# First two column steps of a Fourier projection and of an MLP quarter: weights loaded as 256 by 1024 and multiplied column by column alternately

## The reference

```
sh1, sc1, g1, sh2, sc2, g2 = split(silu(c) @ w_mod + b_mod, 6)
h = modulate(rms_norm(x, norm_g[0]), sh1, sc1)
y = fourier_mix(h) @ fnet_w_out                    # 2048 x 2048
x = x + g1 * rms_norm(y, norm_g[1])
h2 = modulate(rms_norm(x, norm_g[2]), sh2, sc2)
x = x + g2 * rms_norm(square(relu(h2 @ w_mlp_in)) @ w_mlp_out, norm_g[3])   # 2048 -> 8192 -> 2048
```

## Time and profile before

| | us |
|---|---|
| median of 3 runs | 2063.47 (2063.24 to 2064.76) |
| time of the profiled execution | 2066.94 |
| its span | 2064.8 |
| PE busy in it | 2008.3 |
| DVE busy in it | 1437.5 |

### The profile page before, as it was taken

The page is one execution under the profiler, slowest core; times in us unless marked ns, Lnnn a source line. Parts: engine busy times, 40 slices in busy tenths (PEclk is TensorE's granted clock), DMA queues, the critical chain, the costliest instruction groups (busy, mean ns, idle before and its releaser), DMA issues.

```text
span 2064.8 us, 23217 instructions
## 1 busy us (share of the span) xinstructions
PE 2008.3 (97%) x8825; PEld 1628.3 (79%) x8825; DVE 1437.5 (70%) x1507; ACT 1065.6 (52%) x1376; POOL 206.4 (10%) x407
## 2 busy tenths in 40 slices
PE   3999999999999999999999999999999999999998
PEld 1777568888888888888788888888888888888887
DVE  7989867656665555556646566756687887978875
ACT  3333535545444544544666755555555655656554
POOL 0000012001100200200001110000003113031130
PEclk9999999999999999999999999999999999999999
DMA  9999998878866656765555555456656657566573
GB/s 399 402 394 373 352 368 260 293 240 268 284 227 192 215 203 193 222 206 175 173 194 184 176 179 189 160 181 200 229 196 211 227 193 232 197 204 234 193 248 119
DMA packets 210425, 484.41 MB, mean 235 GB/s; under 512 B 17648, under 2 KB 26288, under 8 KB 201488
## 3 DMA queue, kind: packets, MB, share of 16 engines
q1 hardware_dynamic: 196048, 463.25, 65.6%
q0 software_dynamic: 13104, 16.27, 2.7%
q10 hardware_dynamic: 1168, 3.46, 0.4%
HBM read 459.84 MB, written 2.10 MB: 224 GB/s over the span
## 4 chain that ended last, share of the span: by engine, by line
PE 85%; DMA 6%; DVE 6%; ACT 2%; issue 1%; ACTq 0%; DVEq 0%
PE ps L604 23%; PE ps L606 23%; PE ps L605 23%; PE ps L635 4%; PE ps L636 4%; PE ps L634 4%; DVE scr L1672 3%; DMA raw<-in_w_mod 2%; DMA raw<-in_fnet_w 2%; DVE w_low L1659 2%; DMA raw<-in_w_mlp_in 2%; ACT w_high L1148 1%; DVE scr L1687 1%; PE ps L755 1%; PE ps L796 0%
## 5 line engine op out<-in xcount | busy, mean ns | idle before, releaser
L1659 DVE TENSOR_TENSOR w_low<-raw,w_high 128x1024 fp32r<-128x1024 f32 x464 | 563.7, 1222 | 419.9 <-ACT w_high L1148 419.6
L1148 ACT ACTIVATE w_high<-raw 128x1024 fp32r<-128x1024 f32 x464 | 486.7, 1058 | 584.2 <-PE ps L606 480.7
L604 PE MATMUL ps<-w_high,h_both 128*128 128x512 f32 x1152 | 457.4, 397 | 8.8 <-DVE w_low L1659 7.2
L605 PE MATMUL ps<-w_low,h_both 128*128 128x512 f32 x1152 | 450.6, 391 | 0.0
L606 PE MATMUL ps<-w_high,h_both 128*128 128x512 f32 x1152 | 450.5, 391 | 0.0
L604 PE MATMUL ps<-w_high,u_high 128*128 128x512 f32 x1152 | 449.6, 390 | 0.7 <-DVE u_low L2280 0.7
L606 PE MATMUL ps<-w_high,u_low 128*128 128x512 f32 x1152 | 448.6, 389 | 0.0
L605 PE MATMUL ps<-w_low,u_high 128*128 128x512 f32 x1152 | 448.5, 389 | 0.0
L1277 ACT ACTIVATE w_high<-raw 128x1024 fp32r<-128x1024 f32 x232 | 245.2, 1060 | 234.7 <-PE ps L606 117.6
L1862 DVE TENSOR_TENSOR w_low<-raw,w_high 128x1024 fp32r<-128x1024 f32 x232 | 283.1, 1221 | 95.7 <-ACT w_high L1277 91.2
L604 PEld LDWEIGHTS ps<-w_high,h_both 128*128 128x128 f32 x1152 | 217.6, 189 | 58.8 <-DVE w_low L1659 7.7
(11 more groups left out here) (227 smaller groups left out, 1563.9 us busy)
## 6 DMA issues: line engine op xcount, KB each, us to landing
raw<-in_w_mod SPq DMA_DIRECT2D x96, 1024.0 KB, 7.4
raw<-in_w_mlp_in SPq DMA_DIRECT2D x64, 1024.0 KB, 5.7
raw<-in_w_mlp_out SPq DMA_DIRECT2D x64, 1024.0 KB, 5.3
raw<-in_w_up SPq DMA_DIRECT2D x64, 1024.0 KB, 5.1
raw<-in_w_down SPq DMA_DIRECT2D x64, 1024.0 KB, 5.1
raw<-in_w_in SPq DMA_DIRECT2D x48, 1024.0 KB, 5.1
raw<-in_fnet_w SPq DMA_DIRECT2D x16, 1024.0 KB, 7.3
raw<-in_w_out SPq DMA_DIRECT2D x16, 1024.0 KB, 5.0
```

What stands on the lines that cost most here:

```text
L604: eng.matmul(dst, ah, wh, start=(k == first), stop=False)
L605: eng.matmul(dst, ah, wl, start=False, stop=False)
L1148: eng.activation(w_high[:, h % LEAD, :], raw[:, slot, (h % 2) * 2 * CW:(h % 2 + 1) * 2 * CW], ACT.Copy).then_inc(high_ready, 1)
L1659: eng.tensor_tensor(w_low[:, h % LEAD, :], raw[:, slot, piece], w_high[:, h % LEAD, :].bitcast(f32), ALU.subtract).then_inc(raw_used if h ...
```

## The change

For FNET and for the first MLP quarter, column steps 0 and 1 are loaded together: a piece now holds 256 rows by 1024 columns instead of 512 by 512 (`column_pair`), so a contiguous run in memory is 4 KB instead of 2 KB. Each piece is still 1 MB and still gives two halves, but these are now the same two row tiles for step 0 and for step 1. The order of products follows: (0, hh), (1, hh) alternate, so step 0 ends at index 14 of FNET instead of 7, and step 1 at 15 as before. Steps 2 and 3 are as they were. In the MLP, steps 1 and 2 swap banks (4 and 2), and the indices of the blocks and takes move.

```diff
-FIRST_ORDER = [(c, hh) for half in range(2) for c in range(UP_FIRST) for hh in range(4 * half, 4 * half + 4)] + \
+FIRST_ORDER = [pair for half in range(2) for pair in
+               [(c, hh) for hh in range(4 * half, 4 * half + 4) for c in range(2)] +
+               [(2, hh) for hh in range(4 * half, 4 * half + 4)]] + \
               [(c, hh) for c in range(UP_FIRST, NC) for hh in range(HALVES)] + DOWN_ORDER
 FIRST_CHUNKS = [(c, hh // 2) for c, hh in FIRST_ORDER[::2]]
+FNET_ORDER = [(c, hh) for hh in range(HALVES) for c in range(2)] + [(c, hh) for c in (2, 3) for hh in range(HALVES)]
+FNET_ENDS = {FNET_ORDER.index((c, HALVES - 1)): c for c in range(NC)}
+FIRST_PAIRS = {y // 2: hh for y, (c, hh) in enumerate(FIRST_ORDER) if c == 0}
+PAIRED = {y for y, (c, _) in enumerate(FNET_ORDER + FIRST_ORDER) if c < 2}
-FIRST_BANK = (0, 2, 4, 2, 0, 2, 0, 2)
+FIRST_BANK = (0, 4, 2, 4, 0, 2, 0, 2)
-FIRST_TAKES = {y + d: c for c, (y, d) in enumerate(zip(FIRST_UP_ENDS, (5, 6, 7, 6)))}
-FIRST_BLOCKS = {y + d: c for c, (y, d) in enumerate(zip(FIRST_UP_ENDS, (0, 1, 2, 0)))}
+FIRST_TAKES = {y + d: c for c, (y, d) in enumerate(zip(FIRST_UP_ENDS, (4, 7, 7, 6)))}
+FIRST_BLOCKS = {y + d: c for c, (y, d) in enumerate(zip(FIRST_UP_ENDS, (0, 3, 3, 0)))}
...
+            def column_pair(w, hh):
+                load(w[2 * hh * P:2 * (hh + 1) * P, 0:2 * CW].rearrange("(k p) n -> p k n", p=P), 2)
...
             def first_chunk(ch):
+                if ch in FIRST_PAIRS:
+                    column_pair(w_mlp_in, FIRST_PAIRS[ch])
+                    return
...
-                if unit == FNET:
+                if unit == FNET and k < HALVES:
+                    column_pair(fnet_w, k)
+                elif unit == FNET:
                     chunk(fnet_w, k % 4 * 4 * P, k // 4 * CW)
...
-            for c in range(NC):
-                if c >= 2:
+            for y, (c, hh) in enumerate(FNET_ORDER):
+                ch = y // 2
+                if c >= 2 and hh == 0:
                     eng.wait_ge(summed, c - 1)
...
-                eng.activation(w_high[:, h % LEAD, :], raw[:, slot, (h % 2) * 2 * CW:(h % 2 + 1) * 2 * CW],
-                               ACT.Copy).then_inc(high_ready, 1)
+                if h in PAIRED:
+                    eng.activation(ring(w_high, h % LEAD, 2), raw_blocks(slot, EIGHT, h % 2), ACT.Copy)\
+                       .then_inc(high_ready, 1)
...
                 if y < NC * HALVES - LEAD:
                     fnet_high()
-                if y % HALVES == 7:
-                    c = y // HALVES
-                    t.add("done", 8)
+                if y in FNET_ENDS:
+                    c = FNET_ENDS[y]
+                    t.c["done"] = y + 1
                     t.add("summed")
```

More of the change, by code:

```diff
@@ L451, in _ @@
                     mod_tile(G2, MOD_FIRST.index(pos))
-                for c, y in enumerate(FIRST_UP_ENDS):
+                for y, c in FIRST_BLOCKS.items():
                     if pos + 2 == y // 2 + EXCHANGED_BEHIND - 1:
@@ L899, in _ @@
             eng.wait_ge(shift_added, 1)
-            for c in range(NC):
-                if c >= 2:
+            for y, (c, hh) in enumerate(FNET_ORDER):
+                ch = y // 2
+                if c >= 2 and hh == 0:
                     eng.wait_ge(summed, c - 1)
[L903 to L914, removed]
+                if ch == 4 * NC - 1 and y % 2 == 0:
+                    eng.wait_ge(mod_cols, 3)
+                    bias_rows(SC2A)
+                if y % 2 == 0:
+                    t.c["raw"] = AT[FNET, ch]
+                half(2 * (c % 2), hh, h_high, h_low)
+                if y % 2 and ch == GATE_ROWS:
+                    last_read(G1)
+                    sum_partitions_to_rows(G1)
+            t.add("summed", NC)
             for r in range(ROWS_ON_PE):
@@ L940, in _ @@
                 elif hh == 0 and c in (4, 5):
-                    eng.wait_ge(up_taken, 1 if c == 4 else 4)
+                    eng.wait_ge(up_taken, 1 if c == 4 else 3)
                 elif hh == 0 and c > 5:
@@ L1147, in high_part @@
                     eng.wait_ge(half_used, t.at("high", 1 - LEAD))
-                eng.activation(w_high[:, h % LEAD, :], raw[:, slot, (h % 2) * 2 * CW:(h % 2 + 1) * 2 * CW],
-                               ACT.Copy).then_inc(high_ready, 1)
+                if h in PAIRED:
+                    eng.activation(ring(w_high, h % LEAD, 2), raw_blocks(slot, EIGHT, h % 2), ACT.Copy)\
+                       .then_inc(high_ready, 1)
+                else:
+                    eng.activation(w_high[:, h % LEAD, :], raw[:, slot, (h % 2) * 2 * CW:(h % 2 + 1) * 2 * CW],
+                                   ACT.Copy).then_inc(high_ready, 1)
                 t.add("high")
@@ L1658, in low_part @@
                 eng.wait_ge(high_ready, t.at("low", 1))
-                eng.tensor_tensor(w_low[:, h % LEAD, :], raw[:, slot, piece], w_high[:, h % LEAD, :].bitcast(f32),
-                                  ALU.subtract).then_inc(raw_used if h % 2 else low_first, 1)
+                done = raw_used if h % 2 else low_first
+                if h in PAIRED:
+                    eng.tensor_tensor(ring(w_low, h % LEAD, 2), raw_blocks(slot, EIGHT, h % 2),
+                                      ring(w_high, h % LEAD, 2).bitcast(f32), ALU.subtract).then_inc(done, 1)
+                else:
+                    eng.tensor_tensor(w_low[:, h % LEAD, :], raw[:, slot, piece], w_high[:, h % LEAD, :].bitcast(f32),
+                                      ALU.subtract).then_inc(done, 1)
                 t.add("low")
```

## The result

| | before | after |
|---|---|---|
| median, us | 2065.18 (6 runs beside it, 2063.24 to 2067.99) | 2073.29 (6 runs, 2071.74 to 2077.68) |
| ratio | | 1.0037 [1.0026, 1.0049] |
| profiled execution, us | 2066.94 | 2071.74 |
| its span, us | 2064.8 | 2069.9 |

The ratio is worth +7.6 us (2065.2 x 0.0037), with an interval of +5.4 to +10.1. The prediction said +2.7 on a median of 2063.47 (three runs, now 2065.18 over six), and 2069.3 at the most. The sign of the likeliest case held; the time lies outside the range.

The account below looks back on a forecast made before the run. Loads near their limit bounded the first 300 us, with DMA, DVE and PE within a few per cent in the Fourier product; PE bounded the rest. 2.1 + 1.7 - 0.9 - 0.2 = +2.7 us gave 2066.2 us, range 2060.7 to 2069.3.

Parts of the forecast that it names:

- the likeliest case: Fourier half 16: PE's wait outweighs the loads' gain; 2063.5 to 2067.5 us, point 2066.2; chance 0.50.
- The rest ... I take 0: MLP order and step ends: later h tiles and ACT's wait for transposes, about 1 us, change nothing; 0 us.
- With no PE wait of note from 305 us on I take 0.: Behind 305 us: PE's longest group of waits was 1.5 us in all, so this part was priced at 0.
- The end of step 0: Fourier half 16: PE waits 4.7 us for ACT's copy of step 0, making DVE 2.1 us late.
- the 2 to 3 us named as its sign: DVE's scaling of the gate row, 184.39 before: about 2 to 3 us later, likewise PE's row products.
- PE's clock: Behind the wait at Fourier half 16: one half-clock spell costs PE 1.7 us (0 to 3.4).
- The loads: Pair loads at 0.12 us each: eight Fourier loads save 0.9 us, two MLP loads 0.2 us.
- my bounds of 0 to 0.49: Pair loads: saving per load in us, worked out from rates of stretches with mixed run lengths.
- the test that I named: Fourier product: the prediction is wrong if the first product's load rate goes over 405 GB/s.
- (b): Rival on loads: pairs as fast as 8 KB runs; -2.8 us, 2060.7, or 2062.4 with the spell; chance 0.22.
- (c): Rival on PE's late halves: two clock spells, +3.4 us, no load saving; +5.5 us, 2069.0; chance 0.18.
- the last sentence: MLP: the prediction is wrong if PE waits anew there; no size or chance was given.

Follow-up runs that it names:

- copy first: Changed kernel, but ACT copies and squares Fourier step 0 before it rounds half 18; ratio 1.0026, 2071.85 us.
- order only: Changed kernel with 512 by 512 loads in place of the pairs, so wrong weights; ratio 1.0054, 2076.37 us.
- loads only: Kernel before, its order kept, with only the load shapes changed to pairs, so wrong weights; ratio 0.9989, 2064.4 us.
- Both: Changed kernel with exchanges issued one piece earlier on SP and Fourier step 0 copied before half 18 is rounded; ratio 0.9994, 2065.07 us.
- the two mended parts: Against the kernel before: only MLP pairs, exchange one piece earlier, 0.9995, 2065.91 us; only Fourier pairs, step 0 copied before half 18's rounding, 0.9999, 2067.07 us.
- five apart: Changed kernel with earlier exchange and earlier step 0 copy, plus MLP takes five halves behind their blocks; ratio 1.0000, 2066.34 us.

## Why the prediction missed

**"The rest ... I take 0" is the step that failed.** It measures 6.3 us. The prediction set ACT's wait "for DVE's transposes between them, about 1 us, against the four halves of rounding ahead". It left out what happens between the transposes and the take: SP issues eight transfers behind two loads that wait for slots. That gives 4.0 us for SP's waits (342.67 to 346.64), 4.96 for the issues and 3.6 to land, 12.5 us in all where I had counted about 1. Four halves hold 11.0 us of PE's work, and ACT can't use all of them, since it must take, round and hand on before PE comes.

That the takes moved closer to the blocks, and the exchange two pieces back in SP's order, was in the diff. The price, 5 us for eight issues, was in SP's rows of the kernel before (335.11), which the prediction does not use. The experiments show the cause: one piece earlier on SP takes PE's MLP waits from 4.6 us to 0 and the time down by 0.21%, with the distance of four halves left as it is. So the shorter distance alone does not make the loss. Whether SP's place alone would have made it, at five halves, no run shows.

How 19.5 us of waits on ACT become 4.6 on PE is in ACT's rows: 3.20 at 339.49 costs nothing, and only what goes beyond the four halves of lead reaches PE.

**"With no PE wait of note from 305 us on I take 0."** This reason was no reason. It said that PE was covered by ACT's lead, not how large the cover was against the distance that the change shortens. The prediction also reads the slices as "about 200" GB/s from the seventh on. Slices seven to eleven, where these exchanges lie, show 240 to 293, and SP still waits for ring slots there.

**The end of step 0: right, in part by luck.** Wait at half 16 predicted 4.7 us, measured 4.82. Both of its ends lie earlier than worked out, since PE was busy up to it (before, it waited 1.68 us at 149.02): it starts half 16 at 157.81 and not at 159.2. ACT's rounding of half 27 was to run from 184.3 to 185.4; it starts at 186.01, 1.7 us later, since this working leaves out the clock. DVE's scaling, in order of time after:

```profile
187.10 1.23 DVE L1681 TENSOR_TENSOR w_low<-raw,w_high 128x1024 fp32r<-128x1024 f32 x1 [1.43 <-ACT w_high L1165]
188.25 2.48 DVE L1754 TENSOR_TENSOR grow<-ps,grow 128x512 f32<-128x512 f32 x4
...
200.84 1.22 DVE L1775 TENSOR_TENSOR acc<-acc,grow 128x1024 f32<-128x1024 f32 x1
```

It stands 3.9 us behind 184.39, and the gating 3.85 behind 196.99: from there the shift is passed on undiminished, as forecast. Predicted were 2.1 + 1.7 of the clock = 3.8, less the loads; the 2 to 3 us named as its sign leave the clock out. That the sum fits so well is luck in part: PE started 1.4 us earlier than worked out, and the clock cost 1.0 us more. PE's row products carry the shift too. In the chain of the kernel after, in order of time,

```profile
211.49 13.75 PE ps L769 x32
```

they end at 225.24, where they ended at 221.41 before, 3.8 later.

In this one execution the shift is gone by 305 us (304.68 against 305.01), but single executions scatter there by more than the shift. Over the five profiles with the copy behind the rounding, DVE's scaling stands at 187.7 to 189.8 (mean 188.8) and the last continuous stretch starts at 304.7 to 308.1 (mean 306.4). Over the eight without it they are 182.4 to 187.7 (mean 184.8) and 301.6 to 305.4 (mean 303.5). So 4.0 us on the mean become 2.9 by 305 us. The mean price in time, over pairs of kernels, is 3.4 us.

For eleven of the thirteen profiles the span is that start plus PE's waits for `w_low` behind it plus 1759.7 to 1760.7 us, so what comes behind 305 us is fixed but for these waits. The other two have the longest single waits in the MLP, 3.7 us (copy first) and 3.3 us (order only), and stand at 1762.7 and 1762.2. Behind these waits the granted clock falls to 0.69 (360 to 365 us) and 0.66 (365 to 370 us), where it is 1.00 in the changed kernel, whose longest wait there is 2.6 us. So a late exchange can cost the clock as well.

**PE's clock: right in kind, in size on the mean.** The wait is followed by one spell at 1.2 GHz. By stretch, after (clock third from the right):

```profile
158.00:163.00 5.00, 5.00 (x12) 3.95 (x13) 2.70 (x3) 4.60 (x11) 0.00 (x0) 0.50 0.91 329
164.00:170.00 6.00, 6.00 (x28) 4.97 (x27) 3.79 (x3) 2.50 (x3) 0.00 (x0) 1.00 0.82 290
```

The 0.83 and 0.82 of the two stretches of 10 us are parts of this one spell. What it cost is in PE's start of the partition sum, six halves behind half 16, in order of time after:

```profile
176.92 3.59 PE L804 MATMUL ps<-scr,cst 128*128 128x512 f32 x8
```

176.92 - 157.81 = 19.1 us where six halves take 16.4 (6 x 2.74), so 2.7 us against the 1.7 of the sum. In the second execution of the same kernel it is 1.6 us (158.29 to 176.36), in the three other kernels with this wait 1.4 to 2.1. From 290 to 300 us the clock is 0.84 as before, 0.83. What the Trainium skill ("TensorE: Matmul & The Clock Gate", section on the HAM clock gate) says of an idle engine that falls to half clock agrees with the 0.50 behind the wait.

**The loads: right sign, low.** -1.1 was taken, for the ten pair loads that lie on the path; measured were 2.3 us (loads only, 14 pair loads in all) to 3.5 us (changed against order only, 16). That is 0.16 to 0.22 us for each pair load, if all count, or 0.23 to 0.35 for the ten, inside my bounds of 0 to 0.49. I chose the value by a row of 4 KB runs alone (363 GB/s), as the purest. But after the change the same loads move 335 GB/s in that stretch, and the rate from 120 to 150 us wanders between 364 and 411 over kernels with the same loads there. Both bounds were worked out from differences of 5 to 10% between such rates, which one execution can't carry. So the test that I named, above 405 GB/s, tells nothing either: it was passed once (407) and not the second time (387). By "DMA: Bandwidth & Descriptors" of the Trainium skill ("Why small descriptors are slow") the saving would be 0.5 us for eight loads, as the prediction worked out. By the same estimate it is 0.8 us for the 14 loads of "loads only" and 1.0 for 16. The runs show about three times that, but their intervals (0.4 to 4.1, and 3.5 with an uncertainty of 3.4) still contain it.

**Rivals.** (b) did not come: the spell stands behind the wait, and the loads save less. (c) has +3.4 for the clock and ends at 2069.0; the clock cost 2.7 and 1.6 us in two executions, in one spell each, and (c) stops 4 us short of the result. The range's upper end, 2069.3, lies 0.3 above (c), and the 0.19 for "slower, from (c)" above its chance of 0.18; no working gives either. No rival held a new wait in the MLP, only the last sentence did: "or if PE waits anew in the MLP". A failure named as a test deserved a price and a chance.

**What stays open.** "Both" (0.9994), the two mended parts (0.9995, 0.9999) and "five apart" (1.0000) lie above "loads only" (0.9989), whose gain they should show in full. The intervals overlap, so the 1 to 2 us may be chance or a small cost of the alternating order; this was not settled. Open is also how the loss divides between SP's place for the exchange and the shorter distance: no run has one of them without the other, and the earlier issue undoes half of the first. No version beats the kernel before beyond its interval, except the one with wrong weights.

## What to carry to other kernels

When indices move, list for each pair of producer and consumer the distance before and after, and put against it the whole path between them: the queue's waits for other slots, the issue time of every transfer, the landing. Count the place in the issuing queue as one of these distances. A stage without waits tells nothing of how much cover it has; here an exchange two pieces later in SP's order and 2.7 us less distance turned none into 19.5 us on ACT and 4.6 on PE, and one piece earlier took PE's 4.6 away. And a load in a queue that waits for a slot holds up everything behind it: place small transfers that someone soon needs ahead of it.

## What was not expected of the hardware

Eight transfers of 32 KB between SBUF tiles take 4.95 us or more to issue on SP, 0.62 us each, before and after (4.95 to 5.08, and 5.88 once, in the first MLP quarter); eight on POOL take 3.9. ACT could go on 3.3, 3.6 and 4.1 us behind SP's last issue. Single executions of the same kernel differ by 8 us (before: 2061.91 to 2069.56 in 30 runs), in the profiles of the related kernels mostly by what happens between 200 and 305 us. So the time of one profile can't size a difference of 0.2%, though its waits can: these came back within 0.4 us, while the half clock behind the same wait cost 2.7 us once and 1.6 the other time.
